# Attention: how the inverse row sums reach the output tile

## The reference

```python
def forgetting_attention(q, k, v, logf):          # 8 heads of 64, 2048 + 16 tokens
    c = cumsum(logf)
    for i in range(lp // BLOCK):                  # BLOCK = 128 queries
        s = q[i] @ k[:kend].T * scale + c[q0:kend, None] - c[None, :kend]
        p = softmax(where(mask, s, NEG_INF), axis=-1)
        outs.append(p @ v[:kend])
```

## Time and profile before

| | |
|---|---|
| three runs | 2922.24 us median, 2921.28 to 2925.21 |
| profiled execution, span | 2924.8 us, 40628 instructions |
| PE busy | 2840.5 us, 97% |
| DVE, ACT, POOL busy | 1712.9, 616.3, 1350.4 us |
| granted TensorE clock, mean | 0.993 |
| attention loop | 855 to 1352 us |

### The profile page before, as it was taken

How to read it: one execution, slowest core, us unless ns; L and a number is a source line. 1 busy time by engine, 2 the same in 40 slices (tenths; PEclk the granted TensorE clock), 3 DMA queues, 4 the chain that set the end, 5 groups by cost and what they waited for, 6 DMA issues and landing times.

```text
span 2924.8 us, 40628 instructions
## 1 busy us (share of the span) xinstructions
PE 2840.5 (97%) x14442; PEld 2069.8 (71%) x14442; DVE 1712.9 (59%) x4617; ACT 616.3 (21%) x1269; POOL 1350.4 (46%) x1140
## 2 busy tenths in 40 slices
PE   8999999999999999998999989999999999999997
PEld 4478888888875555554455767878877777777775
DVE  6665656656346767674677534777677773332326
ACT  2221212110025454552110100011111111111114
POOL 3433534447730110101355335677667666555645
PEclk9999999999999999999999999999999999999999
DMA  6500110101121103014435456889989989999986
GB/s 219 184 6 1 31 45 1 30 15 44 30 77 35 63 30 129 28 33 170 173 137 159 131 198 197 270 277 277 271 277 289 291 271 302 305 304 305 317 258 254
DMA packets 192571, 470.49 MB, mean 161 GB/s; under 512 B 27384, under 2 KB 108104, under 8 KB 166632
## 3 DMA queue, kind: packets, MB, share of 16 engines
q1 hardware_dynamic: 145424, 347.63, 33.3%
q0 software_dynamic: 44640, 111.84, 16.5%
q10 hardware_dynamic: 2304, 8.39, 0.7%
HBM read 349.64 MB, written 118.11 MB: 160 GB/s over the span
## 4 chain that ended last, share of the span: by engine, by line
PE 39%; DMA 6%; DVE 3%; POOL 2%; issue 2%; SPq 1%; another core or an unknown queue 0%; ACT 0%; DVEq 0%; POOLq 0%; ACTq 0%
PE ps L3021 18%; PE ps L2796 6%; DMA moe_xg<-t_rows,index 5%; PE ps L2969 4%; PE ps L2940 3%; PE ps L2852 2%; DVE moe_xT L2097 2%; PE ps L2937 2%; POOL moe_xg L2523 1%; PE ps L2862 1%; PE ps L2815 1%; POOL moe_fin L2605 1%; PE ps L2806 0%; DMA base_rows<-moe_yo,index 0%
## 5 line engine op out<-in xcount | busy, mean ns | idle before, releaser
L2523 POOL DMA_INDIRECT moe_xg<-t_rows,index x433 | 428.6, 990 | 174.7 <-issue 139.2
L3021 PEld LDWEIGHTS ps<-moe_xT,moe_wg 128*128 128x128 f32 x2048 | 352.5, 196 | 54.6 <-issue 31.3
L3021 PE MATMUL ps<-moe_xT,moe_wg 128*128 128x192 f32 (+22 forms) x2048 | 380.0, 338 | 9.3 <-DVE moe_hh L1997 5.4
L3021 PE MATMUL ps<-moe_xT,moe_wu 128*128 128x192 f32 (+22 forms) x2048 | 376.3, 337 | 0.0
L3021 PEld LDWEIGHTS ps<-moe_xT,moe_wu 128*128 128x128 f32 x2048 | 354.2, 197 | 4.8
L2544 POOL DMA_INDIRECT base_rows<-moe_yo,index x100 | 231.0, 2310 | 273.2 <-DVE moe_yo L2111 116.8
L2097 DVE STREAM_TRANSPOSE moe_xT<-moe_xg 128x256 f32<-128x256 f32 x433 | 235.1, 610 | 174.2 <-DMA moe_xg<-t_rows,index 155.9
L1296 POOL TENSOR_TENSOR fox_diag<-fox_c,fox_causal 128x128 f32<-128x128 f32 x128 | 55.8, 457 | 450.9 <-DVE fox_mx L1325 446.1
L2660 ACT ACTIVATE moe_sl<-ps 128x256 f32<-128x256 f32 (+19 forms) x144 | 49.6, 345 | 953.9 <-PE ps L3021 736.8
L1997 DVE TENSOR_TENSOR moe_hh<-moe_sl,ps 128x256 f32<-128x256 f32 (+19 forms) x144 | 49.7, 358 | 292.4 <-ACT moe_sl L2660 194.9
L1319 DVE CUSTOM_DVE_ANT_0 hT<-ps,fox_c 128x512 f32<-128x512 f32 (+7 forms) x320 | 166.3, 560 | 63.0 <-PE ps L1581 62.7
(11 more groups left out here) (373 smaller groups left out, 5052.1 us busy)
## 6 DMA issues: line engine op xcount, KB each, us to landing
moe_wg<-in_we_gate SPq DMA_DIRECT2D x64, 1024.0 KB
moe_wu<-in_we_up SPq DMA_DIRECT2D x64, 1024.0 KB
moe_wd<-in_we_down SPq DMA_DIRECT2D x64, 1024.0 KB
fox_c<-ck SPq DMA_DIRECT2D x8, 1032.0 KB, 8.9
emb_xin<-in_x SPq DMA_DIRECT2D x16, 512.0 KB, 3.9
h_rows<-emb_hr SPq DMA_DIRECT2D x16, 512.0 KB, 2.7
ret_w<-in_w_in SPq DMA_DIRECT2D x16, 512.0 KB, 6.6
moe_yt<-h_rows SPq DMA_DIRECT2D x16, 512.0 KB
```

What stands on the lines that cost most here:

```text
L2523: pool.indirect_dma_start(out=xg[g % NXG][:, :], out_offset=None, in_=quarters, in_offset=bass.IndirectOffsetOnAxis(ap=route.index4[:, AT4 ...
L3021: ins = pe.matmul(out, w[:, c, f:FF:FC], xT[u][:, c, 0:n], start=(c == 0), stop=(c == DC - 1))
```

## The change

The diagonal matrices, the products with ones, their copy and the four semaphores between them go. DVE's `inverse` keeps the reciprocal only. In the last step of a tile PE also transposes `rinv` (128x4) into four rows of the part of the PSUM bank that this step leaves free; it waits for the reciprocal first. ACT copies these four rows to `rT` ahead of the step's probabilities. SP then issues four DMAs from SBUF to SBUF, each of which reads one row of 128 numbers 64 times and writes it to 64 partitions of `rB`. `finish` waits for these DMAs and for the tile's last `weigh`. In SP's list the store of tile n - 1 and the loads of the next pair now stand in the iteration of tile n, after its `TURN_AT` part and (for tile 17) after `projection_weights`, and the four DMAs of tile n behind them.

```diff
@@ -1172,7 +1172,6 @@
         vp, causal, qk01 = ahead.vp, ahead.causal, ahead.qk01
         sb = Area(nc, "fox", (ahead.small, ahead.small + 2 * 1024 + 1024))
         diag = [sb(f"diag{b}", [P, P]) for b in range(4)]
-        onesf = sb("onesf", [P, FD])
         mx = [sb(f"mx{b}", [P, 2, 8]) for b in range(4)]
         nm = [sb(f"nm{b}", [P, 2]) for b in range(4)]
         rs = [sb(f"rs{b}", [P, 4]) for b in range(2)]
@@ -1184,11 +1183,11 @@
         sb = Area(nc, "fox", (ahead.pairs, ahead.late))
         prob = [[hT[:, 4 * b + r, :] for r in range(4)] for b in range(2)]
         pT = [sb(f"pT{b}", [P, 4, P]) for b in range(4)]
-        rd = [sb(f"rd{b}", [P, 4, P]) for b in range(2)]
+        rT = [sb(f"rT{b}", [4, P]) for b in range(2)]
         rB = [sb(f"rB{b}", [P, QT]) for b in range(2)]
         oT = [sb(f"oT{b}", [P, QT]) for b in range(2)]
         zero = lambda name: ph.zero_sems(name, 1)[0]
-        tab, ones_set = ahead.fox_tab, zero("ones_set")
+        tab = ahead.fox_tab
         w_s, v_s, c_s = ahead.fox_w, ahead.fox_v, ahead.fox_c
         o_s = ahead.fox_out = [nc.alloc_semaphore(name=f"fox_out{b}") for b in range(2)]
         ahead.fox_stored = [16 * (NT // 2)] * 2
@@ -1201,7 +1200,8 @@
         TURN_AT = {TILES * p + x: TILES // 2 * p + x for p in range(PAIRS) for x in range(TILES // 2)}
         scored, biased, bounded, exped, diag_set = (zero(n) for n in ("scored", "biased", "bounded", "exped", "diag_set"))
         turned, pT_a, pT_d, weighed = (zero(n) for n in ("turned", "pT_a", "pT_d", "weighed"))
-        inverted, rd_set, spread, spread_c, scaled = (zero(n) for n in ("inverted", "rd_set", "spread", "spread_c", "scaled"))
+        inverted, rT_set, scaled = (zero(n) for n in ("inverted", "rT_set", "scaled"))
+        rB_in = ph.zero_sems("rB_in", 2)
         block = yield
         w = w_in.rearrange("(c p) n -> p c n", p=P)
         S0, T0, O0 = 0, 4, 6
@@ -1260,6 +1260,21 @@
             sp.wait_ge(added, PRODUCTS * len(FUNITS))
             rows_to_turn(0)
             pair_gates(1)
+            def inverse_rows(n):
+                b = n % 2
+                sp.wait_ge(rT_set, n + 1)
+                if n >= 2:
+                    sp.wait_ge(scaled, n - 1)
+                for q in range(2):
+                    for a in range(2):
+                        sp.dma_start(rB[b][FD * a:FD * (a + 1), P * q:P * (q + 1)],
+                                     rT[b][2 * q + a:2 * q + a + 1, :].unsqueeze(1).to_broadcast([1, FD, P])).then_inc(rB_in[b], 16)
+
+            def store(n):
+                p, t = order[n]
+                sp.wait_ge(scaled, n + 1)
+                sp.dma_start(foxT[2 * FD * p:2 * FD * (p + 1), QT * t:QT * (t + 1)], oT[n % 2][:, :]).then_inc(o_s[n % 2], 16)
+
             for n, (p, t) in enumerate(order):
                 if n in TURN_AT:
                     m = TURN_AT[n]
@@ -1269,11 +1284,14 @@
                         rows_to_turn(m + 1)
                 if n == 2 * TILES + 1:
                     projection_weights()
-                sp.wait_ge(scaled, n + 1)
-                sp.dma_start(foxT[2 * FD * p:2 * FD * (p + 1), QT * t:QT * (t + 1)], oT[n % 2][:, :]).then_inc(o_s[n % 2], 16)
-                if (n + 1) % TILES == 0 and p + 2 < PAIRS:
-                    pair_values(p + 2)
-                    pair_gates(p + 2)
+                if n >= 1:
+                    store(n - 1)
+                if n >= 1 and n % TILES == 0 and p + 1 < PAIRS:
+                    pair_values(p + 1)
+                    pair_gates(p + 1)
+                inverse_rows(n)
+            store(NT - 1)
+
         @block.gpsimd
         def _(pool):
             pool.wait_ge(*ahead.ret_proj)
@@ -1282,7 +1300,6 @@
                     pool.wait_ge(proj, done(g - 2, THIRD))
                 for part in range(4):
                     fox_token_sum(pool, ahead, hT, g, part)
-            pool.memset(onesf[:, :], 1.0).then_inc(ones_set, 1)
             pool.wait_ge(tab, 16)
             for n, (p, t) in enumerate(order):
                 if n % TILES == 0:
@@ -1344,6 +1361,7 @@
                 if s == 0 and not HALF[n]:
                     ins = dve.tensor_copy(dst[0:META, :, :], src[0:META, :, :])
                 elif s == steps[n] - 1:
+                    dve.tensor_copy(rT[n % 2][:, :], src[0:4, 0, :]).then_inc(rT_set, 1)
                     ins = dve.tensor_copy(dst[:, 1:4:2, :], src[:, 1:4:2, :])
                 else:
                     ins = dve.tensor_copy(dst[:, :, :], src[:, :, :])
@@ -1353,13 +1371,8 @@
                 b = n % 2
                 dve.wait_ge(exped, 4 * n + 4)
                 if n >= 2:
-
-                    dve.wait_ge(spread, n - 1)
+                    dve.wait_ge(turned, step0[n - 1])
                 dve.reciprocal(rinv[b][:, :], rs[b][:, :]).then_inc(inverted, 1)
-                dve.wait_ge(inverted, n + 1)
-                for r in range(4):
-                    ins = dve.tensor_scalar(rd[b][:, r, :], ident[:, :], rinv[b][:, r:r + 1], None, ALU.mult)
-                ins.then_inc(rd_set, 1)
 
             def turn_rows(m, g):
                 if g == 0:
@@ -1371,7 +1384,8 @@
 
             def finish(n):
                 b = n % 2
-                dve.wait_ge(spread_c, n + 1)
+                dve.wait_ge(weighed, step0[n + 1])
+                dve.wait_ge(rB_in[b], 64 * (n // 2 + 1))
                 if n >= 2:
                     dve.wait_ge(o_s[b], 16 * (n // 2))
                 dve.tensor_tensor(oT[b][:, :], ps[:, O0 + b, 0:QT], rB[b][:, :], ALU.mult).then_inc(scaled, 1)
@@ -1460,6 +1474,9 @@
                 if s == 0 and not HALF[n]:
                     ins = nc.scalar.copy(dst[0:META, :, :], src[0:META, :, :])
                 elif s == steps[n] - 1:
+                    if n >= 2:
+                        act.wait_ge(scaled, n - 1)
+                    nc.scalar.copy(rT[n % 2][:, :], src[0:4, 0, :]).then_inc(rT_set, 1)
                     ins = nc.scalar.copy(dst[:, 1:4:2, :], src[:, 1:4:2, :])
                 else:
                     ins = nc.scalar.copy(dst[:, :, :], src[:, :, :])
@@ -1476,12 +1493,6 @@
                 nc.scalar.activation(row, row, ACT.Exp, bias=nm[(2 * n + q) % 4][:, a:a + 1],
                                      accum_out=rs[n % 2][:, r:r + 1]).then_inc(exped, 1)
 
-            def keep(n):
-                b = n % 2
-                act.wait_ge(spread, n + 1)
-                if n >= 2:
-                    act.wait_ge(scaled, n - 1)
-                nc.scalar.copy(rB[b][:, :], ps[:, O0 + b, QT:2 * QT]).then_inc(spread_c, 1)
 
             act.wait_ge(*ahead.ret_att)
             act.wait_ge(*ahead.mix_out[0])
@@ -1514,9 +1525,6 @@
                         back(n, s)
                     for q, a in late.get(i, []):
                         exps(n + 1, q, a)
-                    if i == 0 and n >= 1:
-                        keep(n - 1)
-            keep(NT - 1)
 
         @block.tensor
         def _(pe):
@@ -1595,6 +1603,9 @@
                 for a in range(2):
                     if half is None:
                         lo, hi = span(ss[0])
+                        if ss[0] == steps[n] - 1 and a == 0:
+                            pe.wait_ge(inverted, n + 1)
+                            pe.transpose(ps[0:4, T0 + g % 2, 0:P], rinv[n % 2][:, :], ident[:, :])
                         for q in ((1,) if ss[0] == steps[n] - 1 else (0, 1)):
                             r = 2 * a + q
                             ins = pe.transpose(ps[0:hi - lo, T0 + g % 2, P * r:P * (r + 1)],
@@ -1634,15 +1645,6 @@
                                             start=(st == 0 and half == 0), stop=False)
                 ins.then_inc(weighed, 1)
 
-            def scatter(n):
-                pe.wait_ge(rd_set, n + 1)
-                if n == 0:
-                    pe.wait_ge(ones_set, 1)
-                for q in range(2):
-                    for a in range(2):
-                        ins = pe.matmul(ps[FD * a:FD * (a + 1), O0 + n % 2, QT + P * q:QT + P * (q + 1)], onesf[:, :],
-                                        rd[n % 2][:, 2 * q + a, :], start=True, stop=True)
-                ins.then_inc(spread, 1)
 
             for g, (p, i) in enumerate(FUNITS):
                 for which in range(PRODUCTS):
@@ -1671,19 +1673,11 @@
                         weigh(n, s)
                     for u in (per(n + 1, i) if i < lead[n] else []):
                         scores(n + 1, u)
-                if early:
-                    scatter(n)
-                else:
-                    if order[n][1] == 0:
-                        for s in after:
-                            turn(n + 1, s)
-                        scatter(n)
-                    else:
-                        scatter(n)
-                        for u in (range(first[n + 2]) if n + 2 < NT else []):
-                            scores(n + 2, u)
-                        for s in after:
-                            turn(n + 1, s)
+                if not early:
```

(4 more changed lines are left out.)

## The result

| | before | after |
|---|---|---|
| median of 10 runs, us | 2926.44 (2921.28 to 2938.12) | 2940.63 (2937.38 to 2951.45) |
| after / before | | 1.0057 [1.0044, 1.007] |
| profiled execution: span, its own time, us | 2924.8 | 2945.3, 2947.21 |
| attention loop, first transposes of tile 0 to those of tile 31, us | 489.11 | 495.69 |
| from there to PE's first product of the next phase, us | 8.40 | 17.15 |

The kernel became slower by 0.57%. The forecast was 2927.5 us with a range up to 2934, so the time lies outside it, on the side that was thought likelier than the other. The forecast was built on a median of 2922.24 us before the change; over ten runs it is 2926.44, and 4.2 us of the distance come from that. As a difference, +14.2 us was measured and +5.3 forecast, and the range reached to +11.8.

The account below looks back on a forecast made before the run. TensorE (PE) was taken to set the pace, except at the ends of smaller tiles, where it waits for ACT. Sum -4.2 + 7.0 + 0.3 + 2.2 = +5.3 us on 2922.24 gives 2927.5 us, range 2917 to 2934.

Parts of the forecast that it names:

- The gain on PE: Attention loop: removed broadcast products less the added transposes and ACT copies, summed over tiles, gain 4.2 us, bounds 0 and 13.4.
- t = 0: Smallest of a head pair's eight tiles (t = 7 largest): only the added transpose remains, a loss of 0.12 us.
- in the largest tile, where the reciprocal comes latest: Last step of a tile: PE's new wait for the reciprocal costs nothing, as it comes before the last transposes start.
- Tile 17's transfers: Pair 2, t = 6: four transfers queue behind the output weights, PE idles 4.4 us and loses clock; loss 7.0 us, bounds 0 and 9.
- The rival that this stall doesn't come: Tile 17: transfers overtake the weights, or those land sooner; sum -1.7 us, 2920.5 us, chance 0.15.
- Tiles 8 and 16: t = 7 of pairs 1 and 2: transfers land behind the next pair's loads, a tie with DVE's product; loss 0.3 us, bounds 0 and 4.
- The end: End of the attention phase: last product and store wait for store of tile 30, four issues and a landing; loss 2.2 us.
- the broadcasts land late: Rival: landings of 4 us or more, as 64 reads go to one partition; sum +11.3, 2933.5 us, chance 0.22.
- The full gain on PE: Rival: PE gives back its whole 0.42 us in every tile, 13.4 us; 2911.3 us, or 2918.3 with tile 17's stall; chance 0.13.

Follow-up runs that it names:

- d1: Changed kernel with DVE taking the reciprocal ahead of the first two bounds in t = 0 tiles; untimed, t = 0 intervals 11.33 to 11.34 us instead of 11.95.
- a1: Changed kernel with SP issuing tile 17's four transfers ahead of the output weights; 2923.67 us against 2913.06 for the kernel before, ratio 1.0045.
- b1: Changed kernel with the four transfers ahead of the previous tile's store in the last two tiles; ratio to the kernel before 1.0053 (2926.05 against 2913.06 us).
- c1: Changed kernel with transfers reading 64 different rows of the identity instead of one row 64 times; untimed, end 11.92 us instead of 17.15.
- e1b: d1 plus transfers ahead of weights and next pair's loads, in the last two tiles also of the store; ratio to the kernel before 1.001.
- h1: Changed kernel reading one identity row 64 times per transfer, the four rows in partitions 0, 32, 64, 96; untimed, end 15.08 us against 17.15.
- f1b: Changed kernel without the four transfers, rB filled once with ones; 2926.01 us against 2927.04 for the kernel before, ratio 0.9992.
- g1b: Changed kernel with two transfers of twice the width per tile instead of four; untimed, end 17.53 us against 17.15.
- e2c: Repeat run of e1b with the last two tiles done as before the change; 2908.92 us against 2912.09 for the kernel before, ratio 0.999.

## Why the prediction missed

**The gain on PE (forecast -4.2, measured -2.6; without t = 0 forecast -4.6, measured -4.7).** Tile by tile the steps held: t = 6 and 5 gained 0.27 and 0.27 (0.28 forecast), t = 4 and 3 gained 0.13 and 0.17 (0.20), t = 2 0.13 (nothing), t = 1 0.38 (0.40) and nothing in the last pair, t = 7 lost 0.08 (0.12). One step failed: "in the largest tile, where the reciprocal comes latest". It comes latest against the transposes in the smallest one, by 0.89 us. DVE has two bounds ahead of the reciprocal in each tile, and at t = 0 nothing of PE's is long enough to cover them. t = 0 lost 0.70 instead of 0.12; d1 shows the cause.

**Tile 17's transfers (forecast +7.0, measured +7.93).** Place, chain and the loss of the clock were right, and a1 shows that order is the cause. The product started at 1173.92, the forecast said about 1171.8; PE idled 5.52 instead of 4.4 us. I can't put this difference down to the longer landing: with the same transfers d1 lost 6.1 (24.69 - 18.60) and b1 7.7, and c1, with a landing of 1.9 us, lost 6.8, between them. The forecast of 7.0 lies within what one and the same stall took. The rival that this stall doesn't come was wrong.

**Tiles 8 and 16 (forecast +0.3, measured +1.2).** The tie at the product of tile 8 was nearly one; the loss stays within the bounds of 0 and 4 (0.8 to 2.0 us in the runs that keep this order), and it goes when the transfers are issued ahead of the loads (e1b).

**The end (forecast +2.2, measured +8.75).** This is the term that took the time out of the range: of the 10.0 us between +5.3 and +15.3 it makes 6.55, the gain on PE 1.6, tile 18 0.9 and tiles 9 and 17 0.9. The mechanism was named (product, store of tile 30, four issues, landing, product, store), and its two prices were taken from other transfers: 0.38 us for an issue, measured 0.60; 1.9 us for a landing, measured 4.4. Four issues at 0.22 more and 2.5 us of landing make 3.4 us more for a set. Both sets pay it, and as SP holds the second behind `store(30)`, what the first is late is passed on whole. Forecast was the product of tile 30 at 2.2 to 2.6 us behind the first transposes of tile 31; it came at 5.5 (1361.10 - 1355.57), 3.1 later. From there to the last product 3.7 us were forecast and 7.2 measured (1368.29 - 1361.10), 3.5 more. Together that is 6.6, the 6.55 us between +2.2 and +8.75. That the reads of one row are what is slow is shown by c1 (5.2 us of the end; h1, with its rows far apart, gives back 2.1 of them), that the series costs 3.7 by b1; the two overlap, so they aren't added.

**The rival "the broadcasts land late"** had the right kind, the right place (twice at the end) and a landing of 4 us, close to the measured 4.4. It gave 2933.5 with a chance of 0.22: too little weight, since 1.9 us came from rows with another pattern of reading, and too low a price, since it left the issue at 0.38. Between ends as far apart as 1.9 and 4 us, with no row of such a reading, the nearer row was only near in bytes.

**The full gain on PE** didn't come: with no transfer at all (f1b) the loop gained 2.6 of 13.4 us.

## What to carry to other kernels

Moving a small product off a busy engine onto DMAs isn't free at the places where nothing is left to do behind it: count the sets that run in series ahead of a barrier, each with all its issues and its landing, and leave the last tiles on the old way. Before small transfers that an engine waits for are added to a queue, list the bulk that the queue issues within the same stretch and put the small ones ahead of it. A new wait is to be held against the engine's position in the smallest tile, not in the largest, where there is most cover.

## What the runs showed of the hardware

- A DMA from SBUF to SBUF whose source is 64 rows of 512 bytes in 64 partitions landed in 1.9 us (c1), as the store of 128 KB to HBM did; a broadcast that reads one partition 64 times took 3.4 to 4.4 us, and one of 1 KB pieces 5.7. By the Trainium skill, "DMA: Bandwidth & Descriptors" (Latency and other measured facts), HBM is the slowest target; between these two rows, which differ in size and shape, no such difference shows.
- SP took 0.60 us for each of these issues, whether 64 or 4 reads or a single one fell on a partition and whether a piece had 512 bytes or 1 KB; the store takes 0.32 to 0.34.
- At tile 18 PE idled 5.52 us; the granted clock stayed at 1.00 for the first 4.8 us, fell to 0.50 near 1174.7 while PE was still idle, and was back at 1.00 near 1181.3. In the 13.97 us of idle time at the end it fell near 1362.4, 3.7 us in, and in the 4.86 us of the kernel before near 1354.6, 3.2 us in. Where the idle time of tile 18 was gone (a1) so was the fall. It fell in single executions of other kernels as well, with PE at work and less idle time ahead (g1b near 965.3, e2c near 1345.0, each after a wait of under 2 us at the start of its tile).
